# A decoder step on one core: the samples' query projected by itself, key units begun at once, another order of weights, gate products and ring buffers

## The reference, cut to what matters

```python
h  = x + W_out( sig(g_A) * P_A(DSA(xn)) + sig(g_B) * P_B(SB(xn)) ),  xn = RMSNorm(x)
x' = h + HierMoE(RMSNorm(h));  final RMSNorm
# _project: xn @ w_in, split into qa, ka, va, qi, wi, ki, qb, kb, vb, ga, gb
# DSA, on a sample: keys chosen by an index
rel   = relu(einsum('bqhd,bsd->bqhs', q_i, k_i) * IDX_DIM ** -0.5)
score = einsum('bqhs,bqh->bqs', rel, w_i)
_, sel = top_k(score, 256)                 # 64 for the prompt
k_sel, v_sel = cache_k_a[page, sel], cache_v_a[page, sel]
o_a = softmax(q k_sel * HEAD_DIM ** -0.5 + bias_table[t5_bucket(dist)]) v_sel
# SB: stick-breaking over all 2048 cached keys of 8 heads
z = einsum('bqhd,bshd->bhqs', q_b, k_b) * HEAD_DIM ** -0.5
a = exp(log_sigmoid(z) + reverse cumsum of log_sigmoid(-z));  o_b = a v_b
# HierMoE: top-1 of 4 groups, top-2 of its 8 experts, each silu(t w_gate) * (t w_up) then w_down
```

## Time and profile before

| | us |
|---|---|
| median of 3 runs | 668.87 (666.47 to 675.23) |
| the profiled execution: its own time | 667.53 |
| its span in the profile | 665.7 |
| PE busy | 565.5 (85%) |
| PE weight loads, beside it | 320.7 (48%) |
| DVE busy | 370.2 (56%) |
| ACT busy | 136.9 (21%) |
| POOL busy | 127.8 (19%) |

### The profile page before, as it was taken

One profiled execution on the slowest core, in us unless ns is written; L12 is line 12 of the kernel. 1 busy time (PEld: TensorE's weight loads), 2 busy tenths in 40 slices (PEclk: granted clock), 3 DMA queues, 4 the chain that ended last, 5 costly groups with the idle time before them and its releaser, 6 DMA issues.

```text
span 665.7 us, 7505 instructions
## 1 busy us (share of the span) xinstructions
PE 565.5 (85%) x2900; PEld 320.7 (48%) x2900; DVE 370.2 (56%) x672; ACT 136.9 (21%) x267; POOL 127.8 (19%) x116
## 2 busy tenths in 40 slices
PE   3999889989999669878979997799898797989582
PEld 1775567867888634536468444332222222223120
DVE  4079899999999998820323144727243250524034
ACT  3014401125111154441610031110101101010112
POOL 1634231111112877771000000000000000000001
PEclk9997989999999578995999999799999998999898
DMA  9999659798864958999569973379999999999941
GB/s 325 409 369 376 251 192 344 290 386 295 306 262 142 375 167 316 423 411 377 194 167 410 383 312 121 133 240 419 419 420 419 421 419 421 419 420 420 419 189 69
DMA packets 66319, 213.83 MB, mean 321 GB/s; under 512 B 15380, under 2 KB 17956, under 8 KB 58093
## 3 DMA queue, kind: packets, MB, share of 16 engines
q1 hardware_dynamic: 52108, 137.46, 53.0%
q0 software_dynamic: 11392, 73.41, 28.6%
q10 hardware_dynamic: 2784, 2.51, 1.1%
HBM read 208.76 MB, written 4.60 MB: 321 GB/s over the span
## 4 chain that ended last, share of the span: by engine, by line
PE 45%; DVE 26%; SPq 9%; DMA 7%; ACT 6%; issue 4%; ACTq 1%; POOL 1%; DVEq 0%
PE PS L616 7%; DVE arena L1703 6%; DVE x_rows L1707 6%; PE PS L1180 6%; SPq L466 6%; DMA arena<-in_w_down 5%; PE PS L1162 5%; PE PS L1075 4%; PE PS L1188 4%; PE PS L1090 4%; PE PS L1228 3%; SPq L471 3%; DVE temp L1758 1%; PE PS L864 1%; DVE temp L1934 1%
## 5 line engine op out<-in xcount | busy, mean ns | idle before, releaser
L616 PE MATMUL PS<-xT,arena 128*128 128x264 f32 x608 | 142.7, 393 | 0.7 <-ACT arena L1345 0.4
L616 PEld LDWEIGHTS PS<-xT,arena 128*128 128x128 f32 x608 | 114.9, 192 | 25.3 <-issue 4.6
L1703 DVE TENSOR_TENSOR arena<-arena,x_rows 128x2048 f32<-128x2048 f32 x32 | 73.1, 2283 | 20.8 <-ACT x_rows L1297 20.7
L1707 DVE TENSOR_REDUCE x_rows<-arena 128x32 f32<-128x2048 f32 x32 | 73.2, 2287 | 1.1
L546 POOL DMA_INDIRECT arena<-in_cache_k_b,unit_idx x32 | 42.8, 1338 | 140.0 <-DVE x_rows L1707 136.2
L2206 DVE TENSOR_TENSOR x_rows<-PS,x_rows 128x512 f32<-128x512 f32 (+1 forms) x48 | 33.0, 687 | 35.4 <-PE PS L1188 35.2
L1180 PE MATMUL PS<-arena,temp 128*32 128x512 f32 x384 | 45.8, 610 | 4.3 <-issue 3.2
L606 POOL TENSOR_TENSOR small<-small,consts 128x1 f32<-128x1 f32 x3 | 2.6, 868 | 242.7 <-DVE small L2269 242.7
L1228 PE MATMUL PS<-arena,temp 128*32 128x512 f32 x256 | 33.6, 673 | 17.4 <-DMA arena<-in_w_down 13.6
L1188 PE MATMUL PS<-temp 128*128 128x512 f32 (+1 forms) x96 | 45.7, 610 | 1.1 <-DVE temp L2230 1.1
L546 POOL DMA_INDIRECT arena<-in_cache_v_b,unit_idx x32 | 32.8, 1025 | 30.2 <-PE PS L1020 14.7
(11 more groups left out here) (374 smaller groups left out, 799.6 us busy)
## 6 DMA issues: line engine op xcount, KB each, us to landing
arena<-in_w_down SPq DMA_DIRECT2D x32, 1024.0 KB, 17.0
arena<-in_w_gate SPq DMA_DIRECT2D x48, 512.0 KB, 14.2
arena<-in_w_up SPq DMA_DIRECT2D x48, 512.0 KB, 14.7
arena<-in_w_in SPq DMA_DIRECT2D x9, 2048.0 KB, 9.8
temp<-in_w_gate SPq DMA_DIRECT2D x12, 512.0 KB, 15.4
temp<-in_w_up SPq DMA_DIRECT2D x12, 512.0 KB, 15.3
temp<-in_w_out SPq DMA_DIRECT2D x1, 4096.0 KB, 14.7
x_rows<-in_x_prompt SPq DMA_DIRECT2D x2, 1024.0 KB
```

The costliest lines, as they stand in the source:

```text
L616: last = nc.tensor.matmul(PS[0:m, n % 2, 0:T], w[:, k, c0:c0 + m], xT[:, k, :], start=(k == 0), stop=(k == KC - 1))
L1703: nc.vector.tensor_tensor(k_ring[:, u], k_ring[:, u], q_all[:, b % 2:b % 2 + 1, :].to_broadcast([P, 4, H * HD]), ALU.mult).then_inc(s_mul, 1)
L1707: nc.vector.tensor_reduce(z_s[:, b, :].rearrange("p (h r) -> p r h", r=R)[:, 4 * u:4 * u + 4, :], k_ring[:, u].rearrange("p r (h d) -> p r ...
```

## The change

**Start.** The 8 samples' rows, the page table and the first 292 columns of the constants are loaded first; the samples are normed and turned ahead of the prompt. Their QB comes from narrow products of their own: the samples' xT, padded to 32 columns (`xs_pad`), by the 512 QB columns, eight products in four row groups (four partial sums of two, in 32 partitions each, `four_q`); spread_q now sums the four (`pick_q`, from the constant "fold"). Unit 0's keys are fetched ahead of the norm's power on POOL. The bias product of the prompt's table stands behind the turns, and the bias blocks behind the fourth unit on DVE.

**Order of the chunks.** QI 0 to 3, KI 4, QB 5 to 8, KA 9, VA 10, QA 11 to 14, KB 15 to 18, VB and gates as before. One QB chunk stands ahead of the index stage and three behind. The counts stand one or two chunks elsewhere. pad_qa stands behind round 6. Gate 12 follows the prompt's scores, gates 13 to 15 follow list_buckets.

**V ring.** V units n % 8 < 4 go to the key ring, the others to the V ring; fetch_v 0 to 3 wait for the key units, and the wait for all 39 chunks stands behind them, ahead of the clear. The weights w_pa and w_pb lie in the key ring's half, and the first quad's experts are loaded in the order 2, 0, 1, 3.

**Prompt.** Score and logit products go in the order 0, 4, 1, 5, 2, 6, 3, 7.

**Experts.** The first half product of quad i + 1 stands ahead of down(i). The last quad's down weights go to the place of first halves, with a semaphore of their own, and wait only for down(5).

The core of the diff:

```diff
-        v_slot = lambda n: (k_ring if n % 8 >= 4 else v_ring)[:, n % 4]
+        v_slot = lambda n: (v_ring if n % 8 >= 4 else k_ring)[:, n % 4]
+        xs_pad = pads[:, 256:512].rearrange("p (k m) -> p k m", k=KC)
+        four_q = oaT.rearrange("p k t -> p (k t)")[:, 0:H * HD]
+        pick_q = obT.rearrange("p k t -> p (k t)")[:, 0:NS * P].rearrange("p (b m) -> p b m", b=NS)
+        w_pa = arena[:, 0:4 * D].rearrange("p (k n) -> p k n", k=4)
+        down_at = lambda i: 0 if isinstance(i, int) and i == NQ - 1 else 16 * DE
...
-        N_QI, N_KI, N_QA, N_KA, N_VA, N_KB, N_VB, N_GATE, N_ALL = 4, 8, 9, 13, 14, 15, 19, 23, 39
+        N_QI, N_KI, N_QB, N_KA, N_VA, N_QA, N_KB, N_VB, N_GATE, N_ALL = 0, 4, 5, 9, 10, 11, 15, 19, 23, 39
...
+        PAIRED = (0, 4, 1, 5, 2, 6, 3, 7)
...
+            sp.dma_start(x_rows[0:NS, 2, :], a["x_sample"].rearrange("b o d -> (b o) d")).then_inc(s_xs, 16)
+            sp.dma_start(page_of[:, :], a["pages"]).then_inc(s_page, 16)
+            sp.dma_start(consts[:, 0:FIRST], a["shape_consts"][:, 0:FIRST]).then_inc(s_const, 16)
             sp.dma_start(x_rows[:, 0:2, :], a["x_prompt"][0].rearrange("(t p) d -> p t d", p=P)).then_inc(s_x, 16)
-            sp.dma_start(x_rows[0:NS, 2, :], a["x_sample"].rearrange("b o d -> (b o) d")).then_inc(s_x, 16)
-            sp.dma_start(page_of[:, :], a["pages"]).then_inc(s_page, 16)
+            sp.dma_start(w_a[:, :, :], w_in[:, :, O_QB:O_QB + 512]).then_inc(s_wa, 16)
             sp.dma_start(table33[0:NB, :], a["rel_bias_table"]).then_inc(s_tab33, 16)
-            sp.dma_start(consts[:, :], a["shape_consts"]).then_inc(s_const, 16)
...
-            sp.dma_start(w_a[:, :, :], w_in[:, :, O_QB:O_QB + 512]).then_inc(s_wa, 16)
             sp.dma_start(w_b[:, :, :], w_in[:, :, O_QI:O_QI + 512]).then_inc(s_wb, 16)
...
+            sp.dma_start(consts[:, FIRST:], a["shape_consts"][:, FIRST:]).then_inc(s_const2, 16)
...
-            sp.wait_ge(s_proj, N_QI)
-            sp.dma_start(w_a[:, :, :], w_in[:, :, O_QA:O_QA + 512]).then_inc(s_wa, 16)
             sp.wait_ge(s_proj, N_KI)
             sp.dma_start(w_b[:, :, 0:256], w_in[:, :, O_KA:O_KA + 256]).then_inc(s_wb, 16)
+            sp.wait_ge(s_proj, N_KA)
+            sp.dma_start(w_a[:, :, :], w_in[:, :, O_QA:O_QA + 512]).then_inc(s_wa, 16)
+            sp.wait_ge(s_proj, N_QA)
+            sp.dma_start(w_b[:, :, :], w_in[:, :, O_KB + 512:O_KB + 1024]).then_inc(s_wb, 16)
             sp.wait_ge(s_browc, 1)
             sp.dma_start(bias_dram.rearrange("(q r j) -> q r j", q=P, r=H),
                          bias_row.unsqueeze(1).to_broadcast([P, H, 2 * NP_TOK])).then_inc(s_bdram, 16)
-            sp.wait_ge(s_proj, N_KA)
+            sp.wait_ge(s_proj, N_KB)
             sp.dma_start(w_a[:, :, :], w_in[:, :, O_KB:O_KB + 512]).then_inc(s_wa, 16)
-            sp.wait_ge(s_proj, N_KB)
-            sp.dma_start(w_b[:, :, :], w_in[:, :, O_KB + 512:O_KB + 1024]).then_inc(s_wb, 16)
...
-                sp.wait_ge(s_down, i * 2)
+                sp.wait_ge(s_down, i * 2 if i + 1 < NQ else i * 2 - 2)
                 for k in range(4):
-                    down(experts[k], k)
+                    down(experts[k], k, down_at(i), s_wd if i + 1 < NQ else s_wdl)
...
-                elif n >= 4:
-                    pool.wait_ge(s_kused, 4 * NS - 7 + n)
+                elif n < 4:
+                    pool.wait_ge(s_kused, 4 * NS - 3 + n)
...
+            pool.wait_ge(s_const, 16)
+            pool.wait_ge(s_idx, 4)
+            fetch_k(0)
...
-                    fetch_k(k)
+                    if k:
+                        fetch_k(k)
...
-            pool.wait_ge(s_proj, N_ALL)
             for n in range(4):
                 fetch_v(n)
+            pool.wait_ge(s_proj, N_ALL)
             nc.gpsimd.memset(a_pads[0], 0.0).then_inc(s_apad0, 1)
...
+                nc.tensor.matmul(PS[:, 2 + m % 2, :], pick_q[:, b, :], four_q, start=True, stop=True).then_inc(s_tr, 1)
...
+            pe.wait_ge(s_xT, 1)
             pe.wait_ge(s_wa, 16)
-            pe.wait_ge(s_browc, 1)
-            for n in range(4):
-                chunk(w_a, n * P, n)
-            pe.wait_ge(s_evac, 4)
-            for c in range(4):
-                last = nc.tensor.transpose(PS[0:NS, 2 + M_Q % 2, c * P:(c + 1) * P], qbT[:, c, NP_TOK:T], ident)
+            for k in range(KC):
+                rows = slice(k % 4 * 32, k % 4 * 32 + 32)
+                last = nc.tensor.matmul(PS[rows, 2 + M_Q % 2, :], xs_pad[:, k, :], w_a[:, k, :],
+                                        start=(k < 4), stop=(k >= 4))
             last.then_inc(s_tr, 1)
...
+            turn_x(0)
             pe.wait_ge(s_pick, 1)
             spread_q(0)
+            turn_x(1)
+            pe.wait_ge(s_buck, 16)
+            pe.wait_ge(s_ones33, 1)
+            nc.tensor.matmul(PS[:, 0, :], table_wide[:, :], prompt_buckets, start=True, stop=True).then_inc(s_brow, 1)
+
+            pe.wait_ge(s_xT, 5)
             pe.wait_ge(s_wb, 16)
-            for c in range(4):
+            pe.wait_ge(s_browc, 1)
+            for c in range(3):
                 chunk(w_b, c * P, N_QI + c)
             spread_q(1)
+            chunk(w_b, 3 * P, N_QI + 3)
             pe.wait_ge(s_wki, 32)
             chunk(w_ki, 0, N_KI, HD + H)
...
+            project_qb(0)
...
+            pe.wait_ge(s_wb, 32)
+            chunk(w_b, 0, N_KA)
+            count_above(1)
+            spread_q(4)
+            chunk(w_b, P, N_VA)
+            count_above(2)
+            pe.wait_ge(s_wa, 32)
+            chunk(w_a, 0, N_QA)
             chunk(w_a, P, N_QA + 1)
-            count_above(0)
+            count_above(3)
             chunk(w_a, 2 * P, N_QA + 2)
             chunk(w_a, 3 * P, N_QA + 3)
-            count_above(1)
-            spread_q(4)
-            pe.wait_ge(s_wb, 32)
-            chunk(w_b, 0, N_KA)
-            count_above(2)
-            chunk(w_b, P, N_VA)
+            count_above(4)
             pe.wait_ge(s_wa, 48)
             chunk(w_a, 0, N_KB)
-            count_above(3)
             chunk(w_a, P, N_KB + 1)
+            count_above(5)
+            spread_q(5)
...
-            gate(13)
-            gate(14)
+            gate(10)
             list_before()
-            gate(15)
+            gate(11)
             list_told()
             prompt_a_scores(0)
+            gate(12)
             after_keys(0)
             new_key()
             list_buckets()
+            gate(13)
+            gate(14)
+            gate(15)
...
+            def down(i):
+                if not isinstance(i, int) or i + 1 < NQ:
+                    pe.wait_ge(s_wd, i * 64 + 64)
+                elif i + 1 == NQ:
+                    pe.wait_ge(s_wdl, 64)
+                else:
+                    pe.wait_ge(s_wd, i * 64)
...
+            def quad(i, b, use):
+                if not isinstance(i, int) or i:
+                    returned(i)
+                turn_back(i)
+                collect(i + 1)
+                pe.wait_ge(s_second, i * 128 + 128)
+                gate_up(1).then_inc(s_gu, 1)
+                turn(i + 1)
+                turn_hid(i)
+                begin(i + 1, b, use)
+                down(i)
...
+            def last_quad(i):
+                returned(i)
+                turn_back(i)
+                pe.wait_ge(s_second, i * 128 + 128)
+                gate_up(1).then_inc(s_gu, 1)
+                turn_hid(i)
+                pe.wait_ge(s_btc, i + 1)
+                pe.wait_ge(s_add, i * 6)
+                down(i)
...
-                if i == 1:
+                if i == 6:
                     pad_qa()
```

305 lines of the change are left out of this document (156 added, 149 removed).

## The result

The changed kernel takes 696.2 us (median of 4 runs, 692.8 to 698.2), the kernel before 668.6 on the same chip: 1.0392 times as long, with a 95% interval of 1.0329 to 1.0455. Its profiled execution took 695.7 us, its span 693.9. Forecast were 681, with a range up to 690.

What follows compares the result with a forecast made beforehand. Bounds: DVE's 32 key units, then POOL's issue queue to the last gather, then expert weight transfers. 667.5 - 8.9 (start) + 10.1 (KB's weights) + 14.7 (gates, POOL) - 2.2 (experts) = 681.2, say 681 us; range 667 to 690.

Steps and rivals of the forecast that it cites:

- ninth unit: Start of DVE's ninth key unit, which needs sample 2's spread query: from 77.32 to 68.4, -8.9 us.
- sixth answer: DVE's read of PE's sixth count, behind KB's first two chunks: at 132.8, after DVE waits 10.1 us.
- product over the gathered values: PE's product (L861) that waits for the last gather POOL issues: near 317 instead of 301.38, +14.7 us.
- a wait for the small ki/wi weights: PE's wait ahead of the index stage, which it reaches at 37: nothing to 3, taken as 1.5 us.
- part 1: The start, samples' query first: first unit near 21 instead of 36.5, ninth unit earlier by 8.9 us (6 to 11).
- KB's wait: PE waits for KB's weights, loaded into the buffer QA's last chunk frees; DVE waits 10.1 us, 6.3 to 12.7.
- Part 3: Late gates and POOL's order: clear and first K gather wait for all 39 chunks; +14.7 us, 11 to 20.
- rival A: The weight wait costs DVE nothing, by quick landing and unseen slack in the order; 671 us, chance 0.2.
- The tail: Experts' end: last down weights no longer wait for down(6), down(7) at 641.3 instead of 643.46; -2.2 us (0 to -4).
- Rival B: POOL's late gathers hold nothing, or the V stretch makes up in bandwidth; 656.4 if the weight wait hides too; chance 0.07.
- C: Front changes by nothing: POOL takes the start's gain back, or DVE isn't brought forward; only tail left, 665, chance 0.1.
- D: Bias write shares the queue of KB's load, clock stays low through the gates, PE becomes the bound; above 690, chance 0.08.

Runs made afterwards that it cites:

- e6_tail_only: Kernel before with only the change's experts part (next half product ahead of down, last down weights in the place of first halves); 667.3 us, ratio 0.9973.
- e15_before_two: Kernel before with two V gathers instead of one behind each V fetch from the ninth on, fetches 9 to 16; 671.0 us, ratio 1.0018.
- e2_swap_buffers: Changed kernel with KB's weights loaded into w_b and VB's into w_a, so KB's load is issued when VA is done; 677.2 us, ratio 1.0139.
- e13_part3_undone: e12_ki_again with gates 10 to 15 ahead of the list, V ring, POOL's order, w_pa, w_pb and experts' load order as before; 670.2 us, ratio 1.0012.
- e7_ki_by_act: e2_swap_buffers with the two w_ki loads issued by ACT behind its squares instead of by SP behind w_b; 674.4 us, ratio 1.0072.
- e12_ki_again: Same kernel as e7_ki_by_act, run again as a base on another chip; 673.1 us, ratio 1.0051.
- e1_ki_first: Changed kernel with SP issuing both w_ki loads directly behind w_a, ahead of the table, buckets and w_b; 692.7 us, ratio 1.0367.
- e9_before_two: Same kernel as e15_before_two, run on a chip where the kernel before took 685.9 us; 683.3 us, ratio 0.9989.

## Why the prediction was wrong

| step | forecast | profile after | more |
|---|---|---|---|
| ninth unit | 68.4 | 75.20 | 6.8 |
| sixth answer | 132.8 | 142.39 | 9.6 |
| last unit done | 234.3 | 245.18 | 10.9 |
| first K gather | 245.8 | 257.10 | 11.3 |
| ninth V fetch | 268.3 | 280.88 | 12.6 |
| product over the gathered values | 317.3 | 330.29 | 13.0 |
| last down product | 657.2 | 671.79 | 14.6 |

The direction and the places were right: slower, one wait of DVE near the sixth answer, POOL's clear waiting for PE, the product late. The size was half. In the order of the table:

1. The term that failed most is "a wait for the small ki/wi weights, ... from nothing to 3, I take 1.5". It was 8.41 us. In the kernel before, the second load was issued at 11.1 and landed 28.7 us later, at 39.8:

```profile
L436 SPq DMA_DIRECT2D w_ki<-in_w_in x1: 5049/5049/5049, 11.1 to 11.1; - x1
...
DMA to landing us min/median/max: 28.7/28.7/28.7
```

   I had PE there at 37 (it came at 39.6). So the 3 is what the old landing leaves: I took the landing as fixed, though the change puts earlier key fetches and w_ki into the same 48 us of full transfers, and it moved to 48.0. Four profiles of the same code show 3.8 to 8.4 us of waiting. Everything else of part 1 held: with w_ki out of the way the ninth unit starts at 65.5 to 68.1 in the seven profiles of kernels in which ACT loads it, on the chips with 668.6 to 669.2 us (forecast, without the 1.5: 66.9). The start to compare it with moves too: 77.32 in the kernel before, but 74.90 in e6_tail_only and 74.79 in e15_before_two, the same code up to there. Ahead of the first unit four chunks went, not three, and the narrow products took 3.64 us, not 1.8; it started at 23.35, inside its range.

2. KB's wait was named with its place and cause, and mis-sized: forecast 10.1 with 12.7 as its end, measured 12.90 on DVE, and 15.2 us at the end by the profiles. Of the 2.8 us, 1.56 are a wait for QA's weights at 106.94 that I didn't have, since QA's load too is issued, at 97.07, only 8.3 us before PE is ready for it, and lands after 9.8; KB's landing took 11.5 us instead of 9.8. The two chunks behind the wait took 8.95 instead of 7.37, 1.6 more where 1.8 were forecast. (The 5.51 us row that the prediction quotes for this stood behind narrow products; this one stands behind a wait.) The other 2 us come later, by the profiles of the two kernels less the 5.1 that w_ki makes: 1.0 before the list is told, and 1.5 in gate 12, which takes 5.83 us here and 4.36 in e2_swap_buffers. The 6.8 us that the prediction works out from the Trainium skill ("DMA: Bandwidth & Descriptors", section "Anatomy of one DMA") rest on a fit for DMAs that GpSimd issues, and this load is SP's; as an estimate they were further off than the median row. The transfers moved 411 GB/s meanwhile, 4.1 MB in ten us, twice this load's bytes.

3. Part 3's +14.7 came out at the place and in the size that was forecast (K gather, V fetch and product drift by only 2 us between the last unit and the product), but its meaning was wrong. I added it to the front's gain as if the two could be had apart. Undone alone it is worth 3 us at the most seen (e13_part3_undone), because PE then delays DVE by 8.89. The change's front and its late gates are one trade worth +3 to +5 us net; that is rival A's sum, 671, and e7_ki_by_act and e12_ki_again are at 1.0072 and 1.0051, which is 672 to 674. So rival A's number is what the change costs once both weight waits are mended, though not by its reason: the wait for KB was real.

4. The tail: forecast -2.2, in the changed kernel's profile -0.6 from the product on. "The transfers are continuous" held, to the last bytes. SP's issue of the last second halves, and windows behind it (as above; GB/s last):

```profile
646.84 0.34 SPq L473 DMA_DIRECT2D arena<-in_w_gate  x1
...
645.00:650.00 5.00, 3.94 (x34) 1.71 (x30) 1.96 (x8) 1.67 (x3) 0.00 (x0) 1.00 1.01 414
...
655.00:660.00 5.00, 2.88 (x18) 0.77 (x7) 0.69 (x1) 0.25 (x1) 0.00 (x0) 0.87 1.01 408
660.00:665.00 5.00, 5.00 (x10) 1.46 (x9) 2.90 (x5) 0.00 (x0) 0.00 (x0) 0.79 1.02 418
```

   The last down weights were issued right behind these, as forecast, and landed 24.9 us behind 646.84, where both need 20 for their 8.4 MB: 9.6 MB moved in that time, so loads issued earlier were still on their way. From the first expert product to the last down product it took 210.9 us, before 212.2, so the experts gave 1.3 (in e6_tail_only 1.8); and from the product over the gathered values to the first expert product 0.7 more than before, for which the forecast had nothing. Why the experts gave 1.3 and not 2.2 stays open.

5. Rival B (the late gathers hold nothing, or the V stretch makes up for it) falls with the product at 330.29, 2.71 us idle for the last gather, and with e2_swap_buffers; C with the front's size. D's number, over 690, was right, and not by its account: the largest part of the 14.6 us in the last row of the table, 6.8, is w_ki's. The bias write was issued at 105.69 and landed 19.5 us later, so it was still open for the first 3.5 us of KB's load, which landed 1.7 us later than the median of the earlier trace rows; what it cost was not tried, since e2_swap_buffers issues KB's load ahead of it.

What stays open: how much of w_ki's lateness comes from the key fetches that now start earlier. The traces have a hint: in the two profiles with the late landing POOL issued its fifth key fetch at 32.5 and 32.3, in the two with the early one at 35.0 and 35.4. A kernel that holds the keys back was not tried.

## What to carry to other kernels

When an engine is let start earlier, take the landing times of all small loads behind it from the trace, not only its own arrival: the earlier consumer also starts transfers earlier, and here a load of a thousand small pieces at the end of a queue slipped from 39.8 to as late as 48.0. With two weight buffers, the set that is used next must lie in the other buffer than the set in use; two sets in a row in one buffer cost a whole load here, 11.46 us on PE and 12.90 on DVE, which waits for that count. And before adding up a front's gain and a rear's price, ask whether one is bought with the other: undo the rear alone in thought, and see who is late then.

## What was not expected of the hardware

- The second of w_ki's two loads, 1024 pieces each, landed between 42.8 and 48.0 us in four profiles of the same code. SP was held 7.1 and 5.5 us by issuing the two, ACT 0.4 and 0.6. It is not the load alone: in e1_ki_first, where less stood ahead, SP's first issue took 0.58 us and the second 7.95.
- The narrow products took 3.64 us for 16 records, at 15.38, right behind 5.70 us of idling, where the earlier trace rows have 32 such records in 3.64. The profile grants the full clock there. The window:

```profile
15.00:20.00 5.00, 4.62 (x21) 1.73 (x22) 0.22 (x1) 0.60 (x1) 3.58 (x4) 1.00 1.07 414
```

  The four turns behind them took 1.78 us, the next four 1.04. So the first products behind this idling ran at what looks like the lower of the two levels (1.2 GHz), though the row says 1.00. The Trainium skill, "TensorE: Matmul & The Clock Gate", part on the HAM clock gate, gives the lower level as the state of an engine that has been idle; the durations agree, the column doesn't show it. It cost the narrow products 1.8 us.
- POOL issues an indirect DMA every 1.25 us where nothing holds it (0.94 busy, 0.30 between), whether it moves 1 MB or 64 KB. 33 of them are 41 us, which is nearly the whole way from the ninth V fetch to the last gather.
- One chip of the set took 685.9 us for the kernel before where the others took 668.6 to 669.2. In the experts' stretch (440 to 630 us) e9_before_two moved 391 GB/s there, the same kernel on another chip (e15_before_two) 417.
